# Experts' down product in three one-pass terms, two raw down buffers, gathers one expert earlier

## The reference, cut to what matters

```python
h = jax.nn.silu(jnp.einsum('bsd,edf->bsef', x, w_gate)) * jnp.einsum('bsd,edf->bsef', x, w_up)
h = h * combine[..., None].astype(h.dtype)
return jnp.einsum('bsef,efd->bsd', h, w_down)
```

## Time and profile before

| | us |
|---|---|
| median of 3 runs | 2255.76 (2254.35 to 2257.14) |
| the profiled execution | 2259.02 |
| its span, first to last instruction | 2257.2 |
| experts of layer 0, first gather to last home | 485.7 to 685.8 |
| experts of layer 1, first gather to last home | 1195.4 to 1399.9 |

### The profile page before, as it was taken

The page is one execution under the profiler, slowest core; times in us unless marked ns, Lnnn a source line. Parts: engine busy times, 40 slices in busy tenths (PEclk is TensorE's granted clock), DMA queues, the critical chain, the costliest instruction groups (busy, mean ns, idle before and its releaser), DMA issues. The chain is left out here.

```text
span 2257.2 us, 22072 instructions
## 1 busy us (share of the span) xinstructions
PE 1786.8 (79%) x7850; PEld 1327.3 (59%) x7850; DVE 1105.5 (49%) x1627; ACT 803.2 (36%) x1192; POOL 671.4 (30%) x349
## 2 busy tenths in 40 slices
PE   4987885858991897888676897199778486999997
PEld 3864631656660784553465665178558465888885
DVE  2924554646665563556555664664266323242241
ACT  2234565125551333555414453322445223111111
POOL 2324523201110441652401111044342032444442
PEclk9998997859995898999777999599879887999998
DMA  4210021058852411011108783231000013222221
GB/s 163 75 67 1 2 74 38 19 211 341 315 205 105 150 65 39 1 47 29 56 38 337 291 308 134 107 128 59 1 18 1 19 56 131 94 93 100 105 74 46
DMA packets 40473, 233.80 MB, mean 104 GB/s; under 512 B 9316, under 2 KB 9700, under 8 KB 20660
## 3 DMA queue, kind: packets, MB, share of 16 engines
q1 hardware_dynamic: 31012, 215.42, 25.4%
q0 software_dynamic: 9216, 16.80, 2.0%
q10 hardware_dynamic: 144, 0.26, 0.1%
HBM read 226.00 MB, written 23.23 MB: 110 GB/s over the span
## 5 line engine op out<-in xcount | busy, mean ns | idle before, releaser
L2124 POOL TENSOR_TENSOR WS<-ring,WS 128x2048 fp32r<-128x2048 f32 x32 | 154.6, 4832 | 228.5 <-ACT WS L2116 228.5
L249 PE MATMUL bank<-XS,WS 128*128 128x512 f32 x864 | 200.1, 394 | 19.8 <-POOL WS L395 19.8
L249 PEld LDWEIGHTS bank<-XS,WS 128*128 128x128 f32 x864 | 164.2, 191 | 55.4 <-POOL WS L395 21.1
L1206 PE MATMUL bank<-WS,XS 128*128 128x512 f32 x768 | 193.2, 409 | 1.8 <-DVE XS L1311 1.8
L2145 PE MATMUL bank<-XS,WS 128*128 128x512 f32 x768 | 177.2, 393 | 14.2 <-POOL WS L2124 14.2
L2163 PE MATMUL bank<-WS,US 128*128 128x512 f32 x768 | 174.7, 389 | 0.0
L2145 PEld LDWEIGHTS bank<-XS,WS 128*128 128x128 f32 x768 | 145.8, 190 | 44.9 <-issue 14.4
L1206 PEld LDWEIGHTS bank<-WS,XS 128*128 128x128 f32 x768 | 149.4, 198 | 33.7 <-DVE XS L1311 2.6
L2116 ACT CAST WS<-ring 128x2048 fp32r<-128x2048 f32 x32 | 61.2, 1913 | 283.2 <-PE bank L2145 150.0
L2163 PEld LDWEIGHTS bank<-WS,US 128*128 128x128 f32 x768 | 144.1, 188 | 29.9
L1509 PE MATMUL bank<-XS,WS 128*128 128x512 f32 (+1 forms) x600 | 138.4, 393 | 13.9 <-POOL WS L1563 13.9
(11 more groups left out here) (461 smaller groups left out, 3377.8 us busy)
## 6 DMA issues: line engine op xcount, KB each, us to landing
raw<-in_w_exp SPq DMA_DIRECT2D x16, 2048.0 KB, 10.7
DN<-in_w_exp SPq DMA_DIRECT2D x32, 1024.0 KB
ring<-in_w_ff SPq DMA_DIRECT2D x32, 1024.0 KB, 4.7
raw<-in_w_in SPq DMA_DIRECT2D x20, 1024.0 KB, 4.8
GU<-in_w_exp SPq DMA_DIRECT2D x8, 2048.0 KB, 10.6
XT<-in_w_exp SPq DMA_DIRECT2D x8, 2048.0 KB, 10.4
ring<-in_w_in SPq DMA_DIRECT2D x12, 1024.0 KB, 4.8
raw<-in_w_out SPq DMA_DIRECT2D x8, 1024.0 KB, 4.8
```

What stands on the lines that cost most here:

```text
L249: last = pe.matmul(m.ps[g % 8][:, :], WS[:, i % 2, hw, at:at + P], XS[:, hx, k, :], start=(step == 0), stop=(step == 3 * KD - 1))
L1206: last = pe.matmul(m.ps[2 + e % 2][:, :], r.XS[:, e % 2, hx, 4 * half + k, :], r.WS[:, half, hw, k * S:(k + 1) * S], start=(half == 0 and ...
L2124: pool.tensor_tensor(f.WS[:, q % 2, 1, :], f.ring[:, q % 4, :], f.WS[:, q % 2, 0, :].bitcast(F32), ALU.subtract).then_inc(w_low, 1)
```

## The change

The down product becomes three one-pass terms, as gate and up are. ACT rounds the down weights and the transposed hidden values to float32r (`part_high`, and `HT` part 0), DVE writes their remainders (`part_low`, `HT` part 1), and `down_of` runs 12 matmuls in place of 4. The parts lie in one new buffer `DS` (two parts of 2 x 1024 columns), and `HT` becomes one buffer with two parts. `DN` shrinks from four to two raw buffers. ACT now takes both output halves home, DVE none. SP issues GU 0 and GU 1 first, then in its step e DN(e), once part_low(e-2) is done, and GU(e+2). Table, index and gather run for expert e+4 in step e, in place of e+3; in step 0 they run for both 3 and 4.

```diff
-            for e in range(NE):
-                b = e % 4
-
+            def gate_up_in(e):
                 if e >= 4:
                     sp.wait_ge(w_low, 2 * (e - 3))
...
-                if e >= 4:
-                    sp.wait_ge(down, 2 * (e - 3))
...
+            gate_up_in(0)
+            gate_up_in(1)
+            for e in range(NE):
+                if e >= 2:
+                    sp.wait_ge(down_low, 2 * (e - 1))
+                sp.dma_start(r.DN[:, e % 2, :], m.d["w_exp"][bass.ds(layer, 1), e, :, GU:].rearrange("a p n -> p (a n)")).then_inc(dn_in[e % 2], 16)
+                if e + 2 < NE:
+                    gate_up_in(e + 2)
...
             for e in range(NE):
-                if e + 3 < NE:
-                    gather(e + 3)
+                if e == 0:
+                    gather(3)
+                if e + 4 < NE:
+                    gather(e + 4)
                 scatter(e)
...
             def down_of(e):
-                pe.wait_ge(dn_in[e % 4], 16 * (e // 4 + 1))
-                pe.wait_ge(ht_home, e + 1)
+                pe.wait_ge(ht_low, e + 1)
                 for half in range(2):
                     if e:
-                        pe.wait_ge((ye_act, ye_dve)[half], e)
+                        pe.wait_ge((ye_low, ye_up)[half], e)
+                    n = 0
                     for f in range(2):
+                        if half == 0:
+                            pe.wait_ge(down_low, 2 * e + f + 1)
                         at = f * D + half * S
-                        last = pe.matmul(m.ps[5 + half][:, :], r.HT[:, e % 2, f * P:(f + 1) * P], r.DN[:, e % 4, at:at + S], start=(f == 0), stop=(f == 1))
+                        for hw, hx in TERMS:
+                            last = pe.matmul(m.ps[5 + half][:, :], r.HT[:, hx, f * P:(f + 1) * P], r.DS[:, hw, at:at + S], start=(n == 0), stop=(n == 5))
+                            n += 1
                     last.then_inc(down, 1)
...
-                if e + 3 < NE:
-                    table_of(e + 3)
+                if e == 0:
+                    table_of(3)
+                if e + 4 < NE:
+                    table_of(e + 4)
...
             def out_home(e):
-                act.wait_ge(down, 2 * e + 1)
-                if e >= 2:
-                    act.wait_ge(ye_out[e % 2], 16 * (e // 2))
-                act.copy(r.YE[:, e % 2, 0:S], m.ps[5][:, :]).then_inc(ye_act, 1)
+                for half in range(2):
+                    act.wait_ge(down, 2 * e + half + 1)
+                    if e >= 2:
+                        act.wait_ge(ye_out[e % 2], 16 * (e // 2))
+                    act.copy(r.YE[:, e % 2, half * S:(half + 1) * S], m.ps[5 + half][:, :]).then_inc((ye_low, ye_up)[half], 1)
+
+            def part_high(e):
+                act.wait_ge(dn_in[e % 2], 16 * (e // 2 + 1))
+                if e:
+                    act.wait_ge(down, 2 * e)
+                for f in range(2):
+                    act.copy(r.DS[:, 0, f * D:(f + 1) * D], r.DN[:, e % 2, f * D:(f + 1) * D]).then_inc(down_high, 1)
...
-                act.copy(r.HT[:, e % 2, :], m.ps[4][:, 0:2 * P]).then_inc(ht_home, 1)
+                if e:
+                    act.wait_ge(down, 2 * e)
+                act.copy(r.HT[:, 0, :], m.ps[4][:, 0:2 * P]).then_inc(ht_high, 1)
+                part_high(e)
...
-            def out_home(e):
-                dve.wait_ge(down, 2 * e + 2)
...
+            def part_low(e):
+                for f in range(2):
+                    dve.wait_ge(down_high, 2 * e + f + 1)
+                    cols = slice(f * D, (f + 1) * D)
+                    dve.tensor_tensor(r.DS[:, 1, cols], r.DN[:, e % 2, cols], r.DS[:, 0, cols].bitcast(F32), ALU.subtract).then_inc(down_low, 1)
...
-                if e + 3 < NE:
-                    hot_rows(e + 3)
+                if e == 0:
+                    hot_rows(3)
+                if e + 4 < NE:
+                    hot_rows(e + 4)
...
-                if e + 3 < NE:
-                    index(e + 3)
-                if e:
-                    out_home(e - 1)
+                if e == 0:
+                    index(3)
+                if e + 4 < NE:
+                    index(e + 4)
                 if e + 2 < NE:
                     rows_low(e + 2)
-            out_home(NE - 1)
+                dve.wait_ge(ht_high, e + 1)
+                if e:
+                    dve.wait_ge(down, 2 * e)
+                dve.tensor_tensor(r.HT[:, 1, :], m.ps[4][:, 0:2 * P], r.HT[:, 0, :].bitcast(F32), ALU.subtract).then_inc(ht_low, 1)
+                part_low(e)
```

More of the change, by code:

```diff
@@ L1127, in experts @@
 def experts(nc, m, r, layer):
-    names = ("hot_row", "table_done", "indexed", "dve_step", "xe_in0", "xe_in1", "ye_out0", "ye_out1", "gu_in0", "gu_in1", "gu_in2", "gu_in3", "dn_in0", "dn_in1", "dn_in2", "dn_in3", "row_t", "xe_high", "xe_low",
-             "w_high", "w_low", "gate_up", "silu_done", "hidden", "ht_done", "ht_home", "down", "ye_act", "ye_dve")
+    names = ("hot_row", "table_done", "indexed", "dve_step", "xe_in0", "xe_in1", "ye_out0", "ye_out1", "gu_in0", "gu_in1", "gu_in2", "gu_in3", "dn_in0", "dn_in1", "row_t", "xe_high", "xe_low",
+             "w_high", "w_low", "gate_up", "silu_done", "hidden", "ht_done", "ht_high", "ht_low", "down_high", "down_low", "down", "ye_low", "ye_up")
     with stage(nc, "experts", *names) as (block, sems):
-        hot_row, table_done, indexed, dve_step, xe_in0, xe_in1, ye_out0, ye_out1, gu_in0, gu_in1, gu_in2, gu_in3, dn_in0, dn_in1, dn_in2, dn_in3, row_t, xe_high, xe_low, \
-            w_high, w_low, gate_up, silu_done, hidden, ht_done, ht_home, down, ye_act, ye_dve = sems
+        hot_row, table_done, indexed, dve_step, xe_in0, xe_in1, ye_out0, ye_out1, gu_in0, gu_in1, gu_in2, gu_in3, dn_in0, dn_in1, row_t, xe_high, xe_low, \
+            w_high, w_low, gate_up, silu_done, hidden, ht_done, ht_high, ht_low, down_high, down_low, down, ye_low, ye_up = sems
         xe_in, ye_out = (xe_in0, xe_in1), (ye_out0, ye_out1)
-        gu_in, dn_in = (gu_in0, gu_in1, gu_in2, gu_in3), (dn_in0, dn_in1, dn_in2, dn_in3)
+        gu_in, dn_in = (gu_in0, gu_in1, gu_in2, gu_in3), (dn_in0, dn_in1)
         GU = KD * S
@@ L1145, in _ @@
         def _(sp):
-            for e in range(NE):
-                b = e % 4
+            def gate_up_in(e):
                 if e >= 4:
                     sp.wait_ge(w_low, 2 * (e - 3))
-                sp.dma_start(r.GU[b], m.d["w_exp"][bass.ds(layer, 1), e, :, 0:GU].rearrange("a p n -> p (a n)")).then_inc(gu_in[b], 16)
-                if e >= 4:
-                    sp.wait_ge(down, 2 * (e - 3))
-                sp.dma_start(r.DN[:, b, :], m.d["w_exp"][bass.ds(layer, 1), e, :, GU:].rearrange("a p n -> p (a n)")).then_inc(dn_in[b], 16)
+                sp.dma_start(r.GU[e % 4], m.d["w_exp"][bass.ds(layer, 1), e, :, 0:GU].rearrange("a p n -> p (a n)")).then_inc(gu_in[e % 4], 16)
+            gate_up_in(0)
[6 more added lines that the diff above has]
+                    gate_up_in(e + 2)
         @block.gpsimd
@@ L1168, in scatter @@
             def scatter(e):
-                pool.wait_ge(ye_act, e + 1)
-                pool.wait_ge(ye_dve, e + 1)
+                pool.wait_ge(ye_low, e + 1)
+                pool.wait_ge(ye_up, e + 1)
                 pool.indirect_dma_start(out=m.mixed_dram, out_offset=bass.IndirectOffsetOnAxis(ap=r.TB[:, e, 1:2], axis=0),
@@ L1213, in hidden_t @@
                 if e:
-                    pe.wait_ge(ht_home, e)
+                    pe.wait_ge(ht_low, e)
                 for f in range(2):
@@ L1294, in _ @@
                 act.wait_ge(ht_done, e + 1)
-                if e >= 2:
-                    act.wait_ge(down, 2 * (e - 1))
-                act.copy(r.HT[:, e % 2, :], m.ps[4][:, 0:2 * P]).then_inc(ht_home, 1)
+                if e:
+                    act.wait_ge(down, 2 * e)
+                act.copy(r.HT[:, 0, :], m.ps[4][:, 0:2 * P]).then_inc(ht_high, 1)
+                part_high(e)
             out_home(NE - 1)
@@ L1312, in rows_low @@
                                       r.XS[:, e % 2, 0, at, :].rearrange("p k n -> p (k n)").bitcast(F32), ALU.subtract).then_inc(xe_low, 1)
-            def out_home(e):
-                dve.wait_ge(down, 2 * e + 2)
-                if e >= 2:
-                    dve.wait_ge(ye_out[e % 2], 16 * (e // 2))
-                dve.tensor_copy(r.YE[:, e % 2, S:2 * S], m.ps[6][:, :]).then_inc(ye_dve, 1)
+            def part_low(e):
[3 more added lines that the diff above has]
+                    dve.tensor_tensor(r.DS[:, 1, cols], r.DN[:, e % 2, cols], r.DS[:, 0, cols].bitcast(F32), ALU.subtract).then_inc(down_low, 1)
             def hot_rows(e):
@@ L2376, in build @@
                             r.XS = sbr(nc, c4, "XS", P, 2, 2, KD, P)
-                            r.DN = sb(nc, c4, "DN", P, 4, 2 * D)
+                            r.DN = sb(nc, c4, "DN", P, 2, 2 * D)
                             r.YE = sb(nc, c4, "YE", P, 2, D)
```

(3 more changed lines are left out.)

## The result

The changed kernel takes 2219.34 us (median of 4, 2214.64 to 2220.95) against 2255.06 beside it: ratio 0.9837, 95% interval 0.9820 to 0.9855, so 33 to 41 us faster. The prediction was 2213 (2204 to 2232). Its profiled execution took 2218.65 us, with a span of 2216.5.

The account below looks back on a forecast made before the run. The prediction took PE plus a late gather as the bound. Periods of 9.8 us, less longer starts and ends, gained 19.5 and 23.6 us, together 43.1: 2259.0 to 2215.9, by the median 2213 us, range 2204 to 2232.

Parts of the forecast that it names:

- start to gate_up(2): Stage start: table(4) waits for index(3), so gate_up(1) starts 3.6 us later and gate_up(2) 1.1 us later in each layer.
- gate_up(2) to gate_up(14): Mid-stage: twelve periods, ten at 9.8 us and two without table at 9.4, 116.8 us in each layer.
- gate_up(14) to the last hidden_t: Late stage, two gate_up, two down and a small transpose: 16.8 us in place of 18.1, 1.3 saved.
- the end: After the last hidden_t: nothing covers the parts, 1.8 us more, plus 0.5 for a lower TensorE clock: 2.3 (1.5 to 4).
- rival 1: In mid-stage DVE and ACT become the bound: 0.6 us more over 24 full periods, 14 us, 2227 us; chance 0.13.
- a step that was no mechanism: In the total: the median of the runs taken as 3.3 us below the profiled execution, so 2215.9 becomes 2213.
- 16.5 us of lead: Gathers in mid-stage: issued 16.5 us before they are needed, longest landing seen 13.7, so the steady wait is zero.
- rival 3: Gathers stay on PE's path, a wait of about 1 us remaining: 24 us less gain, 2237 us; chance 0.07.
- Rival 2: Transfers become the bound: at 312 GB/s GU 15 is 12 us late in each layer, 2237 us; chance 0.08.
- tie: Per expert in mid-stage, DVE and PE are equally loaded, at 9.6 to 9.8 us.
- wait for expert 3's list: In step 0 table(4) on PE waits for index(3), written by DVE; gate_up(1) starts 3.6 us later.
- harmless: First loads on SP: GU 1 ahead of DN 0 costs nothing, DN 0 being wanted only after the first hidden_t.

Follow-up runs that it names:

- experiment 2: The kernel before with table, hot_rows, index and gather four experts ahead, down product still float32 with four raw down buffers: 2230.77 us, ratio 0.9883.
- experiment 4: The changed kernel without the down loads of experts 2 to 15 (they use the weights of 0 and 1): 2219.55 us, ratio 0.9831 to the kernel before.
- experiment 5: The changed kernel with one more 128x512 subtraction on VectorE per expert, in front of part_low: 2226.51 us, ratio 0.9854 to the kernel before.
- Experiment 7: The changed kernel with first loads on SP in the order GU 0, DN 0, GU 1: 2219.02 us, ratio 0.9841 to the kernel before.
- experiment 1: The changed kernel with table, hot_rows, index and gather only three experts ahead, one-pass product kept: 2258.25 us, ratio 0.9997 to the kernel before.
- Experiment 8: The changed kernel with the last expert's down parts made early, in the first half of WS: 2211.35 us, ratio 0.9793 to the kernel before.
- experiment 3: The one-pass product with gathers three experts ahead, down weights loaded for experts 0 and 1 only: 2212.73 us, ratio 0.9796 to the kernel before.

## Why the prediction was right

**By stages.** Sizes in us, layer 0 / layer 1, before against after, with the last scatter's issue as the end:

| step | forecast | measured |
|---|---|---|
| start to gate_up(2) | +1.1 / +1.1 | +1.9 / +2.0 |
| gate_up(2) to gate_up(14) | -21.6 / -25.8 | -21.1 / -26.1 |
| gate_up(14) to the last hidden_t | -1.3 / -1.3 | -1.4 / -1.4 |
| the end | +2.3 / +2.3 | +3.3 / +3.6 |
| sum | -19.5 / -23.6 | -17.3 / -21.8 |

**How near it was.** 2219.34 us lies in the stated range, but above the 2208 to 2218 of the forecast by itself. The room up to 2232 had been given for rival 1, which did not come; what filled it was the longer start and end and a step that was no mechanism (below). That these fell inside the range is luck; that the period and the waits came as forecast is not.

**PE's period.** 9.76 us was the sum, 9.76 to 9.79 is measured. The product at 0.231 us for each matmul, taken from gate_up's row, held (L1236 has a median of 389 ns, as the earlier trace rows). Layer 1's stretched gate_ups are gone.

**The gather.** The wait went, as forecast. The reason given for its safety, 16.5 us of lead against the longest landing seen of 13.7, was thinner than it looked: the change itself made landings longer (median 13.5, longest 16.3), and the lead is 16.6 us by the rows. The same bytes pass in less time now; experiment 2, whose loads stand as before and whose period is 10.43 us, has 12.1 already. One wait of 0.51 us in layer 0 shows how near rival 3 was.

**The transfers.** Rival 2 had the loads late at 312 GB/s and in time at 350. From 600 to 640 us the changed kernel moved 374 GB/s, and in experiment 4 a third of the bytes less shortens the periods by 0.02 us.

**ACT and DVE.** part_high was put at 1.03 us and takes 1.08, part_low at 1.22 and takes 1.216. DVE's load was put at 9.6 to 9.8 and is 9.37 by experiment 5, 9.46 by its busy time: rival 1 was 0.3 to 0.4 us away, not on the line as the "tie" had it.

**The start.** The place and the price of the wait for expert 3's list were right (4.97 us on PE; gate_up(1) 3.4 to 4.0 later once the first gather's lateness is taken off). Wrong is the step "harmless" on GU 1 ahead of DN 0: the first gather landed later, and gate_up(0) started 1.4 us later in both layers. Experiment 7 shows the order as the cause of the landing, though not of the total.

**The end.** The forecast had the product start 3.1 us after the last hidden_t's start; it was 3.4. The term that was mis-sized is the 0.5 us for a lower clock: the product took 4.57 and 4.90 us, where the same product behind the same gap took 3.38 with the clock at 1.00 (experiment 1, layer 0), so 1.2 and 1.5. Experiment 8 removes most of the gap, and with it the low clock.

**The median.** The stages gave 39.1 us, 4.0 less than forecast. The other 2.3 us of the miss come from a step that was no mechanism: 3.3 us taken off because the profiled execution before stood that far above its median. The one after stood 0.7 below its own (3.3 + 0.7 = 4.0, less 1.6 by which the rest of the span came out shorter; 0.3 us more outside the span and the rounding up to 2213 nearly cancel). That rest has no cause that the traces show: before layer 0's first table matmul the profile after is 3.4 us shorter, where nothing was changed, and after the second stage it is 1.7 longer.

**The parts do not add.** The forecast reckoned 0.90 us for the product and 1.07 for the gather per expert, "if both really leave the path", and did not say what one is worth without the other. Experiments 1 to 3 show the product's share to be nothing without the earlier gather, unless the loads are lighter, and experiment 2 shows it to be 0.66 us with it.

## What to carry to other kernels

Before making the busiest engine faster, look at what it waits for at the end of each period: where a transfer bound it here, the faster engine only waited longer, in bunches, and lost its high clock as well. A gather's lead must be judged by its landing under the load of the new, shorter period. And look at both ends of the loop: the step that was moved ahead left a wait of 4.97 us in the first step, and the new work that the middle covers lay bare in the last one. Mending both, with the first loads in the old order, was worth some 18 to 22 us over the changed kernel by the ratios.

## What the runs showed of the hardware

A gather of 128 rows lands in 5.2 to 5.5 us (median of a layer) where the DMA share is 0.74 to 0.78 (experiments 3 and 4), in 9.1 at 0.80 to 0.83 with the loads issued 3 us ahead of it (the kernel before), in 12.1 and 13.2 at 0.91 and 0.92 with the loads in the same place (experiment 2), and in 13.5 and 11.3 at 0.93 and 0.94 in the changed kernel. On the whole a landing is later where the engines are fuller, but the rows give no fixed rule: 12.1 to 13.2 us at 0.91 to 0.92, and 11.3 at 0.94. The Trainium skill (DMA: Bandwidth & Descriptors, SWDGE vs HWDGE vs iDMA) says that a DMA engine takes turns between the queues of the two kinds. The first gather, 2 us later where GU's large rows alone are beside it, does not contradict that, and no run here isolates it.

TensorE kept 2.4 GHz over a gap of 1.19 us (experiment 8). In experiment 1 the transposes behind gaps of 2.9 to 6.0 us in mid-stage took 1.75 to 1.97 us in place of 1.03, with a granted clock of 0.50 in the 2 us behind the gap of 3.04. The gap alone does not settle it: behind 3.02 us one last product ran at a granted clock of 1.00 and others at 0.62 to 0.65, and in layer 1 of the kernel before the gate_up behind a gap of 2.08 us took 5.72 us, the one behind 1.99 us 6.69.
